# Output projection and gate as seven block products, the first feed-forward chunk plain, and finer waits between layers

## What is computed

```python
mix = jnp.concatenate([y_da, y_ssd.astype(y_da.dtype), y_gla.astype(y_da.dtype)], axis=-1)   # 256 x 1536
h = h + mix @ w_out[i]
f = rms_norm(h, ffn_norm[i])
h = h + (jax.nn.silu(f @ w_ffn_gate[i]) * (f @ w_ffn_up[i])) @ w_ffn_down[i]                 # width 2816
h = h + jax.nn.sigmoid(h @ ple_w_gate[i]) * (p[i] @ ple_w_proj[i])
```

## Time and profile before

| | us |
|---|---|
| median of 3 runs | 1682.53 |
| lowest, highest | 1682.46, 1684.0 |
| profiled execution, its time | 1682.88 |
| its span, first to last instruction | 1681.2 |
| TensorE busy | 1643.7 |
| VectorE busy | 799.1 |
| ScalarE, GpSimd busy | 183.1, 57.3 |

### The profile page before, as it was taken

One profiled execution on the slowest core, in us unless ns is written; L12 is line 12 of the kernel. 1 busy time (PEld: TensorE's weight loads), 2 busy tenths in 40 slices (PEclk: granted clock), 3 DMA queues, 4 the chain that ended last, 5 costly groups with the idle time before them and its releaser, 6 DMA issues.

```text
span 1681.2 us, 19180 instructions
## 1 busy us (share of the span) xinstructions
PE 1643.7 (98%) x8200; PEld 1048.1 (62%) x8200; DVE 799.1 (48%) x1401; ACT 183.1 (11%) x287; POOL 57.3 (3%) x85
## 2 busy tenths in 40 slices
PE   6999999999999999999999999999899999999996
PEld 3775489974458654999545867887544444444442
DVE  3787276764259852766642666701521222212122
ACT  1321000000104110000001420500100000000000
POOL 2000030000010010000000000000000000000000
PEclk9999999999999999999999999999899999999999
DMA  5542365453443324564535323444899999999994
GB/s 156 196 144 75 134 189 180 151 180 120 175 157 121 121 100 134 180 194 155 190 107 200 116 85 109 167 150 160 340 413 427 426 428 428 426 428 428 427 428 163
DMA packets 116334, 374.49 MB, mean 223 GB/s; under 512 B 9796, under 2 KB 57416, under 8 KB 104216
## 3 DMA queue, kind: packets, MB, share of 16 engines
q1 hardware_dynamic: 112736, 370.36, 57.8%
q0 software_dynamic: 1136, 2.17, 0.6%
q10 hardware_dynamic: 2376, 0.72, 0.2%
HBM read 372.18 MB, written 1.05 MB: 222 GB/s over the span
## 4 chain that ended last, share of the span: by engine, by line
PE 95%; DMA 2%; DVE 1%; ACT 1%; issue 0%; ACTq 0%; POOLq 0%; POOL 0%; SPq 0%; DVEq 0%
PE bank L900 16%; PE bank L1216 12%; PE bank L677 10%; PE bank L625 10%; PE bank L951 8%; PE bank L1259 6%; PE bank L636 6%; PE bank L1085 5%; PE bank L1193 3%; PE bank L1226 3%; PE bank L1025 2%; DMA arena<-in_w_up 2%; PE bank L1015 2%; PE bank L1136 2%; PE bank L644 1%; PE bank L991 1%
## 5 line engine op out<-in xcount | busy, mean ns | idle before, releaser
L1216 PE MATMUL bank<-arena,mix 128*64 128x512 f32 x640 | 167.8, 592 | 2.1 <-DMA arena<-in_w_up 1.9
L625 PE MATMUL bank<-weights,xT 128*128 128x512 f32 x384 | 168.9, 597 | 0.8 <-DVE xT L1556 0.8
L677 PE MATMUL bank<-weights,xT 128*128 128x512 f32 x320 | 139.1, 593 | 2.6 <-ACT arena L1294 2.6
L625 PEld LDWEIGHTS bank<-weights,xT 128*128 128x128 f32 x384 | 72.7, 192 | 88.0 <-issue 86.7
L1216 PEld LDWEIGHTS bank<-arena,mix 128*64 128x64 f32 x640 | 55.0, 137 | 110.4 <-issue 110.4
L900 PE MATMUL bank<-arena 128*128 128x128 f32 x1056 | 121.5, 275 | 0.0
L900 PEld LDWEIGHTS bank<-arena 128*128 128x128 f32 x1056 | 119.7, 192 | 0.0
L2477 DVE TENSOR_TENSOR mix<-mix,bank 128x512 f32<-128x512 f32 x16 | 16.9, 1057 | 207.4 <-PE bank L1216 207.4
L1216 PE MATMUL bank<-weights,mix 128*64 128x512 f32 x384 | 111.9, 592 | 0.0
L677 PEld LDWEIGHTS bank<-weights,xT 128*128 128x128 f32 x320 | 60.0, 190 | 75.9 <-issue 75.9
L636 PE MATMUL bank<-xT,weights 128*128 128x256 f32 x448 | 98.5, 380 | 0.0
(11 more groups left out here) (431 smaller groups left out, 2044.6 us busy)
## 6 DMA issues: line engine op xcount, KB each, us to landing
weights<-in_w_in SPq DMA_DIRECT2D x30, 2048.0 KB, 8.2
arena<-in_w_gate SPq DMA_DIRECT2D x20, 2048.0 KB, 17.3
arena<-in_w_up SPq DMA_DIRECT2D x20, 2048.0 KB, 21.0
arena<-in_w_down SPq DMA_DIRECT2D x20, 2048.0 KB, 22.8
weights<-in_w_gate SPq DMA_DIRECT2D x12, 2048.0 KB, 19.2
weights<-in_w_up SPq DMA_DIRECT2D x12, 2048.0 KB, 20.2
weights<-in_w_ffn_gate SPq DMA_DIRECT2D x22, 1024.0 KB, 5.4
weights<-in_w_ffn_up SPq DMA_DIRECT2D x22, 1024.0 KB, 8.0
```

The source lines that it names most:

```text
L625: ins = mm(b[:, :], xT[:, k, t0 + P * t:t0 + P * t + P], w[:, k, :], start=(k == 0), stop=(k == KD - 1))
L677: ins = mm(banks[i][:, :], lhs(k, t), w[:, k % 4, 512 * half:512 * half + 512], start=(k == 0), stop=(k == last))
L1216: ins = mm(moe_bank[bank][SL * e:SL * e + SL, :], xsE[:, k, SL * e:SL * e + SL], w[e][:, k, :], start=(k == 0), stop=(k == KD - 1), skip_g ...
```

## The change

The output projection becomes three chunks of seven block products (`seven`, `out`, `out_last`), the gate two (`gate`). VectorE makes their sums with `row_sums`: for the output projection one set before the gg product and two after it, for the gate two after n3. Each product has a PSUM tile of its own, so wo and pg take seven tiles instead of four; products of different chunks are interleaved. The transposes of n2, n1 and m1 for t=0 now follow the last product. VectorE puts the parts together as they come and sums the squares by halves of 512 columns (`squares`); `layer_end` does this for the gate, with a sigmoid on ScalarE for each of the four parts, by request (`gate_in`, `gate_sig`).

The first feed-forward chunk is computed plainly (`gate_up_plain`), first for t=0 and later for t=1; its sums and its assembly fall away, and VectorE multiplies straight from PSUM. The other chunks stay as they were. The transposes of t=1 move later: for n2 between the third and fourth plain part, for n1 into the middle of k, for m1 before the fourth part of hf. `half_turned` waits for one transposed half at a time.

```diff
-    ("z", 2), ("daT", 2), ("gg", 2), ("ssdT", 2), ("wo", 4), ("glaT", 2),
-    ("n2", 4), ("ffn", 2 * KF), ("pT", 1), ("dn", 7), ("pp", 4), ("n3", 4), ("pg", 4),
+    ("z", 2), ("daT", 2), ("gg", 2), ("ssdT", 2), ("glaT", 2), ("wo", 7),
+    ("n2", 4), ("ffn", 2 * KF - 2), ("pT", 1), ("dn", 7), ("pp", 4), ("n3", 4), ("pg", 7),
...
+            def seven(tile, name, a, a_sum, w, w_sum, first, last):
+                lhs, rhs = dict(p1=(a(0, 0), w(0, 0)), p2=(a(0, 1), w(1, 0)), p3=(a_sum(3), w(1, 1)), p4=(a(1, 1), w_sum(3)),
+                                p5=(a_sum(0), w_sum(0)), p6=(a_sum(1), w_sum(1)), p7=(a_sum(2), w_sum(2)))[name]
+                k = tile + SEVEN[name]
+                b = claim(k) if first else psum[k % NPS]
+                pairs = w(0, 0).shape[1]
+                for j in range(pairs):
+                    ins = mm(b[:, :], lhs[:, j, :], rhs[:, j, :], start=(first and j == 0), stop=(last and j == pairs - 1))
+                return ins.then_inc(psum_full(k), 1) if last else ins
...
-                turned(T("n1"), 0)
-                tokens_out(T("q"), ch, [0])
-                turn(T("n1"), xn, 1, "xn_ready")
-                tokens_out(T("k"), ch + 1, [0])
-                turned(T("n1"), 1)
-                tokens_out(T("q"), ch, [1])
+                tokens_out(T("q"), ch, [0], ahead=lambda half: half_turned(T("n1"), 0, half))
+                tokens_out(T("k"), ch + 1, [0], ahead=lambda half: turn(T("n1"), xn, 1, "xn_ready") if half else None)
+                tokens_out(T("q"), ch, [1], ahead=lambda half: half_turned(T("n1"), 1, half))
...
-                ch = rows_out(T("wo"), ch, KM, lambda k, t: xcols((k + 8) % KM, t), 4, lambda: turn(T("n2"), xn, 0, "xn_ready"),
-                              ahead={4: gla_turn, 8: lambda: mix_turned("glaT")})
+                def out(j, *names):
+                    for name in names:
+                        ins = seven(T("wo"), name, x_blocks(MIX_AT[j]), lambda s_: hsum[:, j % 2, s_], down_blocks(ch + j, 2), out_sums(j), j == 0, False)
+                    return ins
+                def out_last(j, name):
+                    seven(T("wo"), name, x_blocks(MIX_AT[j]), lambda s_: hsum[:, j % 2, s_], down_blocks(ch + j, 2), out_sums(j), False, True)
+                pe.wait_ge(chunk_full(ch), full_at[ch])
+                out(0, "p2", "p1")
+                mix_turned("ssdT")
+                pe.wait_ge(chunk_full(ch + 1), full_at[ch + 1])
+                out(1, "p2", "p1")
+                pe.wait_ge(sem("out_sums"), n.next("out_sums"))
+                out(0, "p6", "p5", "p3", "p7")
+                mix_turn("glaT", "gla_mix_ready", 1024)
+                pe.wait_ge(sem("out_sums"), n.next("out_sums"))
+                out(1, "p6")
+                out(0, "p4").then_inc(sem("chunks_used"), 1)
+                out(1, "p5", "p3")
+                mix_turned("glaT")
+                pe.wait_ge(chunk_full(ch + 2), full_at[ch + 2])
+                out_last(2, "p2")
+                out_last(2, "p1")
+                pe.wait_ge(sem("out_sums"), n.next("out_sums"))
+                for name in ("p6", "p5", "p3"):
+                    out_last(2, name)
+                out(1, "p7")
+                out_last(2, "p7")
+                out(1, "p4").then_inc(sem("chunks_used"), 1)
+                out_last(2, "p4")
+                ch += 3
+                turn(T("n2"), xn, 0, "xn_ready")
...
+                def gate_up_plain(f, q, t):
+                    b = claim(T("ffn") + f) if t == 0 and q == 0 else psum[(T("ffn") + f) % NPS]
+                    w = slot(ch, KD, 256, 2048 * q)
+                    o = 256 * q + P * t
+                    for k in range(KD):
+                        if f == 0 and q == 0 and k % 4 == 0:
+                            half_turned(T("n2"), t, k // 4)
+                        ins = mm(b[:, o:o + P], w[:, k, P * f:P * f + P], xT[:, k, NM + P * t:NM + P * t + P], start=(k == 0), stop=(k == KD - 1))
+                    if t and q:
+                        ins.then_inc(psum_full(T("ffn") + f), 1)
...
-                turned(T("n2"), 0)
                 pe.wait_ge(chunk_full(ch), full_at[ch])
-                gate_up(0, "p1")
-                gate_up(0, "p2")
+                gate_up_plain(0, 0, 0)
+                gate_up_plain(0, 1, 0)
+                gate_up_plain(1, 0, 0)
+                turn(T("n2"), xn, 1, "xn_ready")
+                gate_up_plain(1, 1, 0)
                 pe.wait_ge(chunk_full(ch + 1), full_at[ch + 1])
-                pe.wait_ge(psum_free(T("ffn") + 4 - NPS), fills(T("ffn") + 4 - NPS))
                 gate_up(1, "p1")
-                turn(T("n2"), xn, 1, "xn_ready")
                 gate_up(1, "p2")
-                turned(T("n2"), 1)
-                for c_ in range(FFN_CHUNKS):
+                for f in range(2):
+                    for q in range(2):
+                        gate_up_plain(f, q, 1)
+                for c_ in range(1, FFN_CHUNKS):
...
+                def gate(c, *names):
+                    for name in names:
+                        ins = seven(T("pg"), name, x_blocks(4 * c), lambda s_: hsum[:, c, s_], down_blocks(ch + c, 2), gate_sums(c), c == 0, c == 1)
+                    return ins
+                for c in range(2):
+                    pe.wait_ge(chunk_full(ch + c), full_at[ch + c])
+                    gate(c, "p2", "p1")
+                for c in range(2):
+                    pe.wait_ge(sem("gate_sums"), n.next("gate_sums"))
+                    gate(c, "p6", "p5", "p3")
+                gate(0, "p7")
+                gate(1, "p7")
+                gate(0, "p4").then_inc(sem("chunks_used"), 1)
+                gate(1, "p4")
+                ch += 2
                 after = TILE["n1", layer + 1] if layer + 1 < DEPTH else TILE["m1"]
-                ch = rows_out(T("pg"), ch, KD, xcols, KD, lambda: turn(after, xn, 0, "xn_ready"))
+                turn(after, xn, 0, "xn_ready")
...
+                if m == 3:
+                    turn(TILE["m1"], xn, 1, "xn_ready")
+                hf_out(m, 0, NM + P, 0)
+            for m in range(4):
+                hf_out(m, NM + P, NTOK, 1)
...
+                copy(p1d, T("pg") + SEVEN["p1"], psum[(T("pg") + SEVEN["p1"]) % NPS][:, :])
+                for t, half in ((0, 0), (0, 1), (1, 1), (1, 0)):
+                    act.wait_ge(sem("gate_in"), n.next("gate_in"))
+                    dst = sg[:, t, 512 * half:512 * half + 512]
+                    act.activation(dst, dst, ACT.Sigmoid).then_inc(sem("gate_sig"), 1)
...
+            def row_sums(a, a_sum, w, w_sum, done):
+                TT(w_sum(0), w(0, 1), w(0, 0), ALU.subtract).then_inc(sem("dve_step"), 1)
+                TT(a_sum(0), a(1, 0), a(1, 1), ALU.add).then_inc(sem("dve_step"), 1)
+                v.wait_ge(sem("dve_step"), n.next("dve_step", 2))
+                TT(w_sum(1), w(1, 1), w_sum(0), ALU.subtract).then_inc(sem("dve_step"), 1)
+                TT(a_sum(1), a_sum(0), a(0, 0), ALU.subtract).then_inc(sem("dve_step"), 1)
+                v.wait_ge(sem("dve_step"), n.next("dve_step", 2))
+                TT(w_sum(2), w(1, 1), w(0, 1), ALU.subtract)
+                TT(a_sum(2), a(0, 0), a(1, 0), ALU.subtract)
+                TT(w_sum(3), w(1, 0), w_sum(1), ALU.subtract)
+                TT(a_sum(3), a(0, 1), a_sum(1), ALU.subtract).then_inc(sem(done), 1)
...
+            def squares(t, half, begin):
+                part = st1[:, 40 + t:41 + t]
+                total = st1[:, t:t + 1]
+                o = 512 * half
+                nc.vector.tensor_tensor_reduce(out=xn[:, t, o:o + 512], in0=h[:, t, o:o + 512], in1=h[:, t, o:o + 512], scale=1.0, scalar=0.0,
+                                               op0=ALU.mult, op1=ALU.add, accum_out=part).then_inc(sem("dve_step"), 1)
+                step()
+                if begin:
+                    TS(total, part, 1.0 / D, EPS, ALU.mult, ALU.add).then_inc(sem("dve_step"), 1)
+                    step()
+                else:
+                    STT(total, part, 1.0 / D, total, ALU.mult, ALU.add).then_inc(sem("power_asked"), 1)
...
+            def layer_end(layer, tile, gain):
+                part = Seven(TILE["pg", layer], [mflat[:, 512 * i:512 * i + 512] for i in range(3)])
+                g_ = lambda t, half: sg[:, t, 512 * half:512 * half + 512]
+                for i in range(4):
+                    v.wait_ge(psum_free(TILE["pp", layer] + i), fills(TILE["pp", layer] + i))
+                part.p1_copied()
+                part.sum_of(g_(0, 0), p1d, "p2")
+                v.sem_inc(sem("gate_in"), 1)
+                part.sum_of(part.u2, p1d, "p6")
+                part.sum_of(part.u4, part.u2, "p5")
+                gated(0, 0)
+                squares(0, 0, True)
+                part.sum_of(g_(0, 1), part.u4, "p3")
+                v.sem_inc(sem("gate_in"), 1)
+                gated(0, 1)
+                squares(0, 1, False)
+                part.plus(part.u3, part.u2, part.landed("p7"))
```

(47 more changed lines are left out.)

253 lines of the change are left out of this document (120 added, 133 removed).

## The result

| | us |
|---|---|
| changed kernel, median of 4 runs | 1667.98 |
| lowest, highest | 1667.48, 1668.89 |
| kernel before, the same chip | 1683.22 |
| ratio, 95% interval | 0.991 (0.9893 to 0.9927) |
| profiled execution, its time and span | 1668.89, 1667.2 |

The page's first block answers to the earlier trace rows: TensorE's busy time fell by 12.0 us, the span by 14.0.

The account below looks back on a forecast made before the run. TensorE, 98% busy, was taken as the bound, so removed matmuls count in full; −5.3 − 3.6 − 4.3 − 0.5 = −13.7 us gave a median of 1668.8 us, range 1665.8 to 1674.

Parts of the forecast that it names:

- Unit prices: TensorE's chain: 0.858 us per matmul of 512 columns, 0.223 us per matmul of 128 columns, paces unchanged.
- Output projection, n2 and feed-forward: Each layer: −5.15 us of matmuls, +1.79 for the plain chunk, +0.7 idle; −2.66 us, twice: −5.3 us.
- weights late: Rival: second feed-forward chunk's weights share bandwidth and land 1.2 us late per layer; 1671.2 us; chance 0.08.
- Layer 0's end: Gate to q: −3.43 matmuls, −1.28 bank wait, +0.4 second weights, +0.1, +0.6 before q; −3.6 us.
- Layer 1's end: Gate and hf: fewer matmuls and waits, less 0.8 and 1.55 us idle at m1's second transposes; −4.3 us.
- Start and middle: Start only: q begins after half the rows are copied out, partly at lower clock perhaps; −0.5 us.
- rival 3: Better: routing stage meets the clock change at another moment, 1 to 3 us either way; good side 1666; chance 0.10.
- given back: Rival: expert stream sets the end, so the gain before the MoE is mostly lost; about 1681 us; chance 0.04.
- Rival 5: Slower clock: TensorE stays at 1.2 GHz after about five idle places, costing 20 us; 1689 us; chance 0.03.

Follow-up runs that it names:

- all5: Changed kernel with five moves together: down projection's last two chunks in sequence, two transposes moved, whole-row squares after the gate, copies before p4; 1663.55 us.
- dn_apart: Changed kernel with the down projection's last two chunks run one after the other, not interleaved; 1666.01 us, 0.9903 of before.
- hf_turn: Changed kernel with m1's transposes for t=1 in the middle of hf's fourth part instead of before it; one run, 1668.38 us.
- u_gate: Changed kernel with gate, claim of its banks and layer end as before the change; 1674.21 us, 0.9946 of before.
- u_half: Changed kernel with TensorE waiting for both transposed halves before starting on the first; 1673.64 us, 0.9939 of before.
- u_out: Changed kernel with TensorE's and VectorE's part of the output projection plain again; 1679.05 us (10 runs), 0.9975 of before.
- u_ffn: Changed kernel with the first feed-forward chunk by seven products again; 1670.51 us, 0.9926 of before.
- all5_seven: The all5 kernel with the first feed-forward chunk by seven products again; 1667.58 us, 0.9908 of before.
- after_again: The changed kernel as it is, run again for comparison on the chip of other runs; 1667.78 us, 0.9911 of before.
- n2_turn: Changed kernel with n2's t=0 transposes before the output projection's last product, copied out before p4 is added; 1666.61 us, 0.9902 of before.

## Why the prediction held, step by step

**Unit prices: held.** The matmuls and the paces are as forecast. D is +1.78 us for 8 matmuls of 128 columns (1.79 by the pace), and the gate of all5 takes 24.03 us for 28 matmuls (0.858 each). The layers as a whole gained 11.6 us, where the three terms below had 13.2.

**Output projection, n2 and feed-forward: held, −2.6 us a layer against −2.66.** C −4.36 and D +1.78 (layer 1 the same). The idle place before the plain chunk is 0.80 us, forecast 0.7, with p4's addition ahead of the copy, as forecast. The third set of sums has 0.35 us in hand, forecast 0.6. The second feed-forward chunk is in time, with no line among the waits, so the rival "weights late" didn't come here.

**Layer 0's end: mis-sized, −2.2 us against −3.6.** The term that was mis-sized is the second gate chunk. I let it land 12.6 us after issue as in the earlier trace rows and put 0.4 of idle. It took 13.67 and TensorE waited 1.30, and around that wait 0.35 us more is lost in small pauses: 1.25 of the 1.4 missed. The gate also starts 0.16 us late. The 0.1 before the transposes is 0.14. The place was right and dn_apart shows the cause; the size wasn't, and why the same pair, again issued within 1 us, took 1.1 us longer than in the earlier trace rows isn't settled. The rival "weights late" was thus right in kind and wrong in place. The 0.6 us before q is 0.66.

**Layer 1's end: held, −4.26 us against −4.3.** The 1.55 us at m1's transposes came as 1.03 before them and 0.47 as the half-wait in hf's first part (hf_turn, u_gate). VectorE was late by the forecast amount, at two places instead of one.

**Start and middle: −1.6 us against −0.5, half of it luck.** A is −0.85. Of this 0.11 is the first transfer, which TensorE waits for until 12.16 instead of 12.27; 0.74 fits q starting on half the rows, and A is 14.34 to 14.67 in every run but before and u_half. B is −0.78 because the first records of q ran at half pace for a shorter time, 2 us instead of 3.5; in the same code that time differs by more than this from run to run (last section). The prediction feared a loss there and got a gain.

**Experts and routing: −0.8 us, not foreseen.** H is +0.92: this execution spent 14 us of it at the granted clock of 0.50, the profiled execution of before 10. That is rival 3, on its bad side. I is −1.73: a wait for in_w_up, in the profiles of before, u_out, u_gate, u_ffn and all5_seven 1.5 us or more (I 469.0 to 469.5), is 0.4 us or less in the others (467.8 to 468.1). What decides between the two stays open. The gain before the experts came through whole, so "given back" falls.

**The sum.** −11.6 us for the layers (−5.2, −2.2, −4.3), +0.1 in q of layer 1, −1.6 for start and middle and −0.8 later make −14.0, the difference of the two profiled executions, against −13.7. The miss at layer 0's end (+1.4) and the gains not forecast (−1.1, −0.8) nearly cancel: the total is nearer than its parts, and that is luck. The medians differ by 15.2; the 1.2 us on top lie in executions without a trace.

**The clock: refuted for idle places of this size.** The granted clock is 1.00 around idle times of 0.44, 0.80, 1.03 and 1.30 us, and from 17 to 1183 us throughout. Rival 5 had priced them at 20 us. The Trainium skill, page "TensorE: Matmul & The Clock Gate", section "A second HAM failure mode: psum-queue depth-cycling", says that frequent micro-idles between groups of matmuls can make the clock swing; this trace shows no swing for a few single idle places, the nearest of them 5 to 8 us apart.

## What to carry to other kernels

When an engine at 98% loses work, the gain is the work less what becomes late next: price it by the pace in the chain, then follow the engine that takes over, instruction by instruction, up to each hand-over; that gave the idle places here to 0.2 us (the two at hf taken together), except where a transfer set the time. For a transfer take the issue time and what is in flight beside it and leave a microsecond or more of doubt on a duration read at another moment. Cover an idle place with neighbouring work (half a part of hf, one product of two matmuls, a plain chunk in place of a Strassen one) before shortening what it waits for.

## What was not expected of the hardware

**The same kernel differs by up to 3.6 us from run to run, and the granted clock goes with it.** after_again took 1665.94, 1669.57, 1666.65 and 1668.91 us at mean clocks of 0.996, 0.994, 0.996 and 0.994. A difference of 0.002 over 1667 us is 3.3 us of clock. In the traced executions it lies in the routing stage, where TensorE is partly idle. The windows of after_again (H 16.93), then of n2_turn (H 20.33), the same code there:

```profile
1180.00:1187.00 7.00, 4.94 (x38) 4.18 (x37) 5.84 (x26) 2.48 (x3) 0.36 (x1) 0.94 1.01 428
1187.00:1194.00 7.00, 4.42 (x24) 4.28 (x25) 3.31 (x18) 0.00 (x0) 0.00 (x0) 0.58 1.01 428
1194.00:1200.00 6.00, 5.73 (x36) 3.26 (x37) 4.46 (x20) 1.50 (x2) 0.00 (x0) 1.00 0.34 143
```

```profile
1180.00:1187.00 7.00, 6.04 (x28) 5.53 (x26) 4.42 (x23) 2.48 (x3) 0.00 (x0) 0.50 1.01 426
1187.00:1194.00 7.00, 3.96 (x17) 3.82 (x18) 3.67 (x19) 0.00 (x0) 0.00 (x0) 0.50 1.00 426
1194.00:1200.00 6.00, 5.73 (x33) 4.42 (x33) 2.84 (x12) 0.55 (x2) 0.00 (x0) 0.80 0.15 61
```

The stage begins at 1179.1 in the one and at 1177.6 in the other. In after_again the clock stood at 0.50 (1.2 GHz) for 7 us of it, in n2_turn for 17, and the stage took 3.4 us more. The other traces fit: 10 us at 0.50 go with H of 17.79 to 18.40, 14 us with 18.85 to 19.42. The mean clock isn't the whole of it: all5's four executions differ by 2.1 us at 0.994 each.

**At the start TensorE runs at half pace, and the view of the clock doesn't say so.** The first 24 records of q take 11.00 us in after_again and 12.59 in all5, from the same code:

```profile
14.42 11.00 PE L646 MATMUL bank<-weights,xT 128*128 128x512 f32 x24
```

```profile
14.58 12.59 PE L646 MATMUL bank<-weights,xT 128*128 128x512 f32 x24
```

From 15 to 18 us, 7 records begin in the one and 3 in the other, while PEclk reads 1.00 in both. Behind its first records q keeps a distance of 0.43 us from one start to the next; before that it is 0.85 us, and 0.96 to 0.99 behind the very first. The change comes at 15.4 us in after_again, 16.5 in the changed kernel, 18.7 in all5 and 18.9 in before. The trace's own record of the granted clock begins at just these times (15.35, 16.51, 18.71, 18.92); for the time before it has no record, and the view prints 1.00 there. So a 1.00 ahead of the first record says nothing, and the pace has to be read from the starts. B less what the long distances cost is 28.44 us, to 0.01, in all fourteen traces: this is all that makes B vary.
